# Retention of a two-layer decoder step: last chunk's transposes behind a swish tile, sample state requested earlier, zero-state products left out

## The reference, cut to what matters

```python
def step(s, qkv):
    qc, kc, vc = qkv
    scores = jnp.einsum('bhqd,bhkd->bhqk', qc, kc) * intra
    o = (jnp.einsum('bhqk,bhkv->bhqv', scores, vc)
         + jnp.einsum('bhqd,bhdv->bhqv', qc, s) * q_decay[None, :, :, None])
    s = (s * chunk_decay[None, :, None, None]
         + jnp.einsum('bhkd,bhkv->bhdv', kc * k_decay[None, :, :, None], vc))
    return s, o
...
o = (o - mu) * lax.rsqrt(var + GN_EPS)
o = (o.reshape(B, L, D_RET_V) * jax.nn.silu(g.astype(f32))).astype(h.dtype)
```

## Time and profile before

| | us |
|---|---|
| runs | 2209.39, 2207.01, 2209.02 |
| median | 2209.02 |
| the profiled execution | 2204.35 |
| its span | 2202.5 |
| TensorE busy | 2098.8 (95%) |
| DVE, ACT, POOL busy | 1124.8, 698.2, 338.6 |

### The profile page before, as it was taken

The page is one execution under the profiler, slowest core; times in us unless marked ns, Lnnn a source line. Parts: engine busy times, 40 slices in busy tenths (PEclk is TensorE's granted clock), DMA queues, the critical chain, the costliest instruction groups (busy, mean ns, idle before and its releaser), DMA issues.

```text
span 2202.5 us, 37914 instructions
## 1 busy us (share of the span) xinstructions
PE 2098.8 (95%) x15356; PEld 2007.0 (91%) x15356; DVE 1124.8 (51%) x1706; ACT 698.2 (32%) x896; POOL 338.6 (15%) x314
## 2 busy tenths in 40 slices
PE   5999899989999999999999999989899999999997
PEld 2899889979998999999989998989899989999997
DVE  5534546886345534343456254488743463535343
ACT  2123433455323212121231244325552331212122
POOL 0001102430013101010230010044100310101014
PEclk9999999999999999999999999999999999999998
DMA  8341242222224333333332213422222422222222
GB/s 332 140 176 58 72 161 93 72 71 78 86 82 167 123 117 115 115 115 115 120 139 78 76 53 111 154 72 72 75 79 87 153 68 87 77 87 80 84 87 97
DMA packets 78918, 232.58 MB, mean 106 GB/s; under 512 B 7360, under 2 KB 27840, under 8 KB 78528
## 3 DMA queue, kind: packets, MB, share of 16 engines
q1 hardware_dynamic: 56304, 204.86, 27.2%
q10 hardware_dynamic: 22480, 25.78, 3.5%
HBM read 218.52 MB, written 12.09 MB: 105 GB/s over the span
## 4 chain that ended last, share of the span: by engine, by line
PE 83%; DVE 10%; ACT 3%; issue 2%; DMA 1%; DVEq 1%; ACTq 0%; POOL 0%; POOLq 0%
PE acc L1161 72%; PE misc L1231 2%; PE acc L1212 2%; DVE taps L869 2%; DVE weight_l L691 1%; ACT weight_h L364 1%; PE misc L1241 1%; DVE tmp L921 1%; PE misc L1350 1%; DVE taps L867 1%; PE misc L1324 1%; PE misc L1322 1%; PE misc L1323 1%; PE misc L1388 1%; DVE tmp L886 0%
## 5 line engine op out<-in xcount | busy, mean ns | idle before, releaser
L364 ACT ACTIVATE weight_h<-raw 128x1024 fp32r<-128x1024 f32 x288 | 304.7, 1058 | 1038.8 <-PE acc L1161 997.1
L1161 PE MATMUL acc<-h_hi,weight_h 128*128 128x288 f32 x2688 | 587.7, 300 | 26.0 <-DVE weight_l L691 20.7
L1161 PE MATMUL acc<-h_lo,weight_h 128*128 128x288 f32 x2688 | 578.5, 297 | 0.0
L1161 PE MATMUL acc<-h_hi,weight_l 128*128 128x288 f32 x2688 | 578.2, 297 | 0.0
L691 DVE TENSOR_TENSOR weight_l<-raw,weight_h 128x1024 fp32r<-128x1024 f32 x288 | 400.4, 1390 | 265.2 <-ACT weight_h L364 265.2
L1161 PEld LDWEIGHTS acc<-h_hi,weight_h 128*128 128x128 f32 x2688 | 435.6, 190 | 42.3 <-DVE weight_l L691 27.6
L1161 PEld LDWEIGHTS acc<-h_lo,weight_h 128*128 128x128 f32 x2688 | 436.5, 190 | 0.0
L1161 PEld LDWEIGHTS acc<-h_hi,weight_l 128*128 128x128 f32 x2688 | 436.0, 190 | 0.0
L1161 PE MATMUL acc<-b_hi,weight_h 128*128 128x288 f32 x1792 | 388.8, 299 | 18.5 <-DVE tmp L939 13.7
L1161 PE MATMUL acc<-b_lo,weight_h 128*128 128x288 f32 x1792 | 385.5, 297 | 0.0
L1161 PE MATMUL acc<-b_hi,weight_l 128*128 128x288 f32 x1792 | 385.2, 297 | 0.0
(11 more groups left out here) (207 smaller groups left out, 1759.9 us busy)
## 6 DMA issues: line engine op xcount, KB each, us to landing
raw<-stream SPq DMA_DIRECT2D x290, 512.0 KB, 3.4
ada_raw<-ada_in SPq DMA_DIRECT2D x84, 512.0 KB, 6.0
s_s<-state_in ACTq DMA_DIRECT2D x8, 1024.0 KB, 5.5
ret_s_out<-s_s ACTq DMA_DIRECT2D x8, 1024.0 KB, 4.9
two_raw<-ada_in SPq DMA_DIRECT2D x12, 512.0 KB, 9.3
x<-x_in ACTq DMA_DIRECT2D x1, 2304.0 KB, 12.9
wrg<-wrg_in ACTq DMA_DIRECT2D x18, 128.0 KB, 2.0
const<-const_in SPq DMA_DIRECT2D x1, 1246.0 KB, 8.6
```

The costliest lines, as they stand in the source:

```text
L364: A(weight_h[:, j % 2, :], raw[:, (j + 2) % 4, :], ACT.Copy).then_inc(h_split, 1)
L1161: last = M(acc[j % 2][:, half, 0:HALF], w, r[:, k, half * HALF:(half + 1) * HALF], start=(k == 0 and n == 0), stop=(k == KT - 1 and n == 2))
```

## The change

- `turn_v` of the last V tile moves behind the scores of the first chunk. Tiles 6 and 7 go through `misc` banks 2 and 3 (`v_bank`), so that banks 0 and 1 are free for the scores.
- `turn_o` of the eighth chunk moves behind the first G tile, and ACT's copy of it (`o_evac`) behind the split that follows that tile. `sample_scores` no longer waits for this copy; `sample_updates` does.
- The state `s_p` moves to the bytes of `taps`, `on_p` behind `v_tok`, and the staging tiles into the second half of `s_s`. ACT requests the first sample state at the start of the MA tiles, the second after the second store, and doesn't wait for the stores.
- `kd_s` lies in the bytes of `taps`, so DVE waits for both stores ahead of it. Ahead of that wait, at all even G tiles, stands now `split_l`.
- For the first chunk of each i there is no product with `s_p` (L1323), no zeroing (L792), and the state is a copy in place of two multiply-adds (L806).
- Two loops of DVE and POOL over i are written out.

```diff
@@ -89,6 +89,11 @@
     return buf[:, bass.ds(m, 1), :].rearrange("p o (a b) -> p (o a) b", a=2)
 
 
+def v_bank(j):
+
+    return 2 if j >= 6 else 0
+
+
 def prompt(tile):
     return tile[:, :, 0:HALF_P]
 
@@ -140,17 +145,17 @@
                    enumerate([offs["qk"] + 2 * TOK * 4 + q * 4096 for q in range(3)] + [offs["side"]])]
         two_row = place("two_row", [128, 512], F32, lo + 4 * 4096)
         x_part = place("x_part", [128, 2, NB_S], F32, offs["side"] + 4096)
-        s_p = place("s_p", [128, 2, DV], F32, lo)
-        on_p = place("on_p", [128, 2, DV], F32, lo + 2048)
-        p_m = place("p_m", [128, 2, CHUNK], F32, lo + 4096)
-        kd_p = place("kd_p", [128, 2, DK], F32, lo + 5120)
-        k_st = place("k_st", [128, 2, 2, CHUNK], F32, lo + 6144)
-        q_st = place("q_st", [128, 2, 2, CHUNK], F32, lo + 8192)
+        on_p = place("on_p", [128, 2, DV], F32, offs["tmp"] + 4 * 4096)
+        p_m = place("p_m", [128, 2, CHUNK], F32, lo + 8192)
+        kd_p = place("kd_p", [128, 2, DK], F32, lo + 9216)
+        k_st = place("k_st", [128, 2, 2, CHUNK], F32, lo + 10240)
+        q_st = place("q_st", [128, 2, 2, CHUNK], F32, lo + 12288)
         s_s = place("s_s", [128, 2, DB, DV], F32, lo)
         k_ss = place("k_ss", [128, NB_S], F32, lo + 16640)
         on_s = place("on_s", [128, DV], F32, lo + 16896)
         wrg = place("wrg", [128, 2, 256])
         taps = place("taps", [128, STRIP])
+        s_p = place("s_p", [128, 2, DV], F32, offs["taps"])
         kd_s = place("kd_s", [128, DB // 2, DK], F32, offs["taps"])
         q_sm = place("q_sm", [128, DB * COLS])
         p_ms = place("p_ms", [128, 128])
@@ -452,8 +457,8 @@
                     split_h(lay, AT_V, 0, j)
                     ada_between(AT_V + j)
                     act.wait_ge(v_turned, lay * 8 + j + 1)
-                    A(v_tok[:, :, j * 128:(j + 1) * 128], misc[:, 0, :].rearrange("p (c d) -> p c d", c=4), ACT.Copy)
-                    A(v_s[0:NB_S, j * 128:(j + 1) * 128], misc[0:NB_S, 1, 0:128], ACT.Copy).then_inc(v_ready, 1)
+                    A(v_tok[:, :, j * 128:(j + 1) * 128], misc[:, v_bank(j), :].rearrange("p (c d) -> p c d", c=4), ACT.Copy)
+                    A(v_s[0:NB_S, j * 128:(j + 1) * 128], misc[0:NB_S, v_bank(j) + 1, 0:128], ACT.Copy).then_inc(v_ready, 1)
 
                 def o_evac(i, c, n):
 
@@ -466,6 +471,12 @@
                     act.wait_ge(s_ready, lay * 8 + (i * 4 + 4) + 1)
                     act.dma_start(ret_p_out[bass.ds(lay * 4 + i * 2, 2)].rearrange("h p n -> p h n"), s_p[:]).then_inc(ret_p_stored, 16)
 
+                def load_state(i, e):
+
+                    act.wait_ge(state_stored[e], lay * 32 + i * 16 + 1)
+                    act.dma_start(s_s[:, e], state_in[bass.ds(lay, 1), :, bass.ds(i * 2 + e, 1)].rearrange("l b h p n -> p (l b h) n")).then_inc(state_loaded[e], 16)
+
+                load_state(0, 0)
                 zero = lay * 0
                 for t in range(8):
                     i, c = t // 4, t % 4
@@ -482,23 +493,16 @@
                     A(gstd[:], mv[:, :, 1], ACT.Sqrt, bias=eps_g[:]).then_inc(gstd_ready, 1)
                     if t == 3:
                         store_state(0)
-                o_evac(zero + 1, 3, n)
                 store_state(1)
 
-                act.wait_ge(ret_p_stored, lay * 32 + 32 + 1)
-
-                def load_state(i, e):
-
-                    act.wait_ge(state_stored[e], lay * 32 + i * 16 + 1)
-                    act.dma_start(s_s[:, e], state_in[bass.ds(lay, 1), :, bass.ds(i * 2 + e, 1)].rearrange("l b h p n -> p (l b h) n")).then_inc(state_loaded[e], 16)
-
-                load_state(0, 0)
                 load_state(0, 1)
                 for i in range(2):
                     for j in range(4):
                         e, m = j // 2, i * 4 + j
                         n = lay * 4 + i * 2 + e
                         split_h(lay, AT_G, zero + i, j)
+                        if i == 0 and j == 0:
+                            o_evac(zero + 1, 3, lay * 8 + 7)
                         if i == 0 and j == 3:
                             load_state(1, 0)
                         if i == 1 and j == 1:
@@ -786,10 +790,7 @@
                         V.tensor_copy(dst[:, SEQ:TOK].rearrange("p (a b) -> p a b", a=2), sample(acc[j % 2])).then_inc(acc_free, 1)
                         split_l(lay, AT_V, i, j)
 
-                with dve.Fori(0, 2) as i:
-                    dve.wait_ge(ret_p_stored, lay * 32 + i * 16 + 1)
-
-                    V.memset(s_p[:], 0.0)
+                for i in range(2):
                     for c in range(4):
                         n = lay * 8 + i * 4 + c
                         dve.wait_ge(scores_ready, n + 1)
@@ -802,7 +803,10 @@
                         V.tensor_copy(one(mix, i * 4 + c), acc[c % 2][:, :, 0:HALF]).then_inc(acc_free, 1)
                         split_l(lay, AT_MA, i, c)
                         dve.wait_ge(o_ready, n + 1 + 1)
-                        for e in range(2):
+                        if c == 0:
+                            dve.wait_ge(ret_p_stored, lay * 32 + i * 16 + 1)
+                            last = V.tensor_copy(s_p[:], misc[:, 2, :].rearrange("p (e d) -> p e d", e=2))
+                        for e in range(2 if c else 0):
                             last = V.scalar_tensor_tensor(s_p[:, e, :], s_p[:, e, :], cdec[:, bass.ds(i * 2 + e, 1)], misc[:, 2, e * 256:e * 256 + 256], ALU.mult, ALU.add)
                         last.then_inc(s_ready, 1)
                         ch = Chain(dve, norm_chain, n * 2)
@@ -828,9 +832,12 @@
                             V.tensor_tensor(apart, misc[0:NB_S, 0, 0:NB_S].rearrange("p (s c) -> p s c", c=2 * DS),
                                             mask_s[:, bass.ds(h, 1), :].rearrange("p o (s c) -> p (o s) c", c=2 * DS), ALU.mult)
                             kt = misc[0:NB_S, 0, 128:256].unsqueeze(1).to_broadcast([NB_S, DB // 2, DK])
+                            split_l(lay, AT_G, i, j)
+                            dve.wait_ge(ret_p_stored, lay * 32 + 32 + 1)
                             km = kdm[:, bass.ds(h, 1), :].rearrange("p o b -> p (o b)").unsqueeze(2).to_broadcast([NB_S, DB // 2, DK])
                             V.tensor_tensor(kd_s[0:NB_S], kt, km, ALU.mult).then_inc(s_masked_ready, 1)
-                        split_l(lay, AT_G, i, j)
+                        if j % 2:
+                            split_l(lay, AT_G, i, j)
                         dve.wait_ge(g_sig, lay * 8 + i * 4 + (j + 1))
                         V.tensor_tensor(one(tmp, m), acc[j % 2][:, :, 0:HALF], one(tmp, m), ALU.mult).then_inc(acc_free, 1)
                         ch = Chain(dve, s_chain, n * 2)
@@ -1070,7 +1077,7 @@
                     for n in range(ADA_PROLOGUE, ADA_JOINT):
                         add_bias(n, lay, n * 4, n % 2)
                     pool.wait_ge(tables_loaded, 16)
-                with pool.Fori(0, 2) as i:
+                for i in range(2):
                     for c in range(4):
                         n = lay * 8 + i * 4 + c
                         pool.wait_ge(qk_ready, lay * 8 + 8 + 1)
@@ -1280,9 +1287,10 @@
                     pe.wait_ge(acc_free, n[0] + (j + 3))
                     pe.wait_ge(v_ready, n[1] + j + 1)
                     src = o_t[:, 2 + j % 2, :]
+                    bank = v_bank(j)
                     for c in range(4):
-                        nc.tensor.transpose(misc[:, 0, c * 128:(c + 1) * 128], src[:, c * 128:(c + 1) * 128], ident)
-                    nc.tensor.transpose(misc[0:NB_S, 1, 0:128], src[:, SEQ:TOK], ident).then_inc(v_turned, 1)
+                        nc.tensor.transpose(misc[:, bank, c * 128:(c + 1) * 128], src[:, c * 128:(c + 1) * 128], ident)
+                    nc.tensor.transpose(misc[0:NB_S, bank + 1, 0:128], src[:, SEQ:TOK], ident).then_inc(v_turned, 1)
 
                 n = (lay * LAYER_TILES + AT_V, lay * 8)
                 for j in range(8):
@@ -1290,7 +1298,7 @@
                     if j:
                         turn_v(n, j - 1)
                     ada_between(AT_V + j)
-                turn_v(n, 7)
+                v_base = n
 
                 def turn_o(n):
 
@@ -1301,8 +1309,6 @@
                             last = nc.tensor.transpose(misc[:, 3, (2 * e + half) * 128:(2 * e + half + 1) * 128], on_p[:, e, half * 128:(half + 1) * 128], ident)
                     last.then_inc(on_turned, 1)
 
-                pe.wait_ge(v_ready, lay * 8 + 8 + 1)
-                carry(pe)
                 for i in range(2):
                     for c in range(4):
                         n = lay * 8 + (i * 4 + c)
@@ -1312,22 +1318,26 @@
                             M(misc[:, 0, e * 256:e * 256 + 128], k_st[:, c % 2, e, :], qc, start=True, stop=True)
                             last = nc.tensor.transpose(misc[:, 0, e * 256 + 128:e * 256 + 256], k_st[:, c % 2, e, :], ident)
                         last.then_inc(scores_ready, 1)
+                        if n == lay * 8:
```

(14 more changed lines are left out.)

## The result

The changed kernel takes 2231.47 us (four runs, 2226.68 to 2235.28) against 2208.61 for the kernel before beside it: 1.010 times as long, 95% interval 1.0076 to 1.0124. It is slower by 22.9 us, where 13.4 were forecast. The profiled execution took 2226.68, 22.3 above that of before.

The account below looks back on a forecast made before the run. TensorE was taken to bound the kernel (83% of the chain). Gains -5.4 - 3.5 - 13.7, stalls +24.8 and clock +11.2 give +13.4 on 2204.35: 2217.8, plus 4.67 to the median, forecast 2222, range 2211 to 2234 us.

Parts of the forecast that it names:

- Last V transposes: At the last V tile, scores fill the wait for ACT's `v_s`: gain 1.9 us in layer 0, 3.5 in layer 1.
- Zero state: TensorE's product with the zero state (L1323) goes, 0.43 us eight times: gain 3.5 us.
- Tail: After the eighth chunk, waits and half clock go: 7.35 us left per layer, gain 13.7 us for both.
- The early request at nothing: ACT's first sample state load, requested at the start of the MA tiles, was costed at nothing.
- The stall: At even G tiles `kd_s` comes behind `split_l`, so `sample_o` starts 3.0 us after the tile: eight times, +24.8 us.
- The restart: TensorE's first products after each wait for `kd_s` run slower, making 3.2 us of each 3.0 us gap.
- DVE's later work behind the split: DVE's sigmoid product, statistics and state update come later, but answer to a tile ending 6.4 us after: nothing charged.
- Faster: Rival: the wait for `kd_s` behind `split_l` is only about 2.0 us with no clock fall: 2202 us; chance 0.07.
- The clock: TensorE's clock falls to half behind seven of the eight new waits, at 1.6 us each: +11.2 us.
- the rival of long falls: Every clock fall lasts the longer time, as `sample_o` and updates are small products: 23.2 us, total 2234; chance 0.11.

Follow-up runs that it names:

- the run with the late request: Changed kernel with `kd_s` made ahead of `split_l` again, and the first sample state requested behind the second store: 2191.94 us.
- the run with the wait filled: Changed kernel with three 512-column matmuls, their result overwritten, ahead of each of the eight waits for `kd_s`: 2212.15 us, ratio 1.0019 to the kernel before.
- the version with `kd_s` first: Changed kernel with `kd_s` made ahead of `split_l` at even G tiles again: 2186.47 us, ratio 0.9894 to the kernel before.
- the swap alone: Kernel before with only `split_l` put ahead of `kd_s` at even G tiles: 2257.37 us, ratio 1.0217 to the kernel before.

## Why the prediction was right, and by how much its terms were off

The mechanism and the direction were right; the measured 2231.5 lies within 2211 to 2234, near its upper end. Point by point:

**Last V transposes.** Forecast 1.9 and 3.5 us. The chain of after in layer 0, then in layer 1, against the earlier trace rows:

```profile
180.34 0.12 PE misc L1293
...
182.12 6.38 PE acc L1168 x48
```

```profile
1266.52 0.12 PE misc L1293
...
1268.29 6.38 PE acc L1168 x48
```

From the end of tile 6's transposes to the MA tile 1.66 and 1.65 (forecast 1.58), in place of 3.50 and 4.21, and the MA tile of layer 1 takes 6.38 in place of 7.23. Gain 1.8 and 3.4. Right.

**Zero state.** Eight times 0.43. Right by the rows.

**Tail.** From the eighth chunk's end to the end of `turn_o` 7.31 us in both layers (261.69 to 269.00, 1347.87 to 1355.18), forecast 7.35. Right; taking it back cost 15.8 where 13.7 were put.

**The early request at nothing: wrong.** The step named its cover rightly for the weight tiles, but judged the state's own landing by its 6.7 us being "far earlier than needed" and so priced the move at nothing. The run with the late request shows waits of 2.9 us (5.5 us in all by the medians, not clear of their scatter): the price of a cover that another part of the same change takes away. It didn't alter the sum, as the tail's gain had been booked in full.

**The stall.** Forecast T + 3.0, measured 3.04 six times and 2.61 twice: 23.5 us. The restart was put at 0.2 each; `sample_o`'s first pair takes 0.67 in place of 0.63, so it is 0.04. The term is 23.8 in place of 24.8. DVE's later work behind the split, put at nothing, cost nothing: in the run with the wait filled, the next G tile takes its 6.58.

**A slip without weight.** In the rival *Faster*, eight stalls of 2.0 with `turn_o` in two of them are 15.2, not 15.6.

**The clock: the term that was mis-sized.** Seven falls at 1.6 were put; the profiled execution has six, and their price, as excess over the same rows without a fall (0.67, 1.00, 1.06 and 6.58), is 1.4 at 315, 3.0 at 335, 3.1, 3.1 and 3.1 in layer 1, and 1.6 at 1431: 15.3 in place of 11.2. The step that was mis-sized is "I take the shorter, since TensorE has work at once behind each new stall". The work at once is the small products of `sample_o` and `sample_updates`, and the slow stretch began in or behind them and lasted nearly 7 us in four of six times. That was the rival of long falls, at 0.11; the truth lies between it and the forecast. By medians the term is 19.3 (the filled kernel), which the scatter doesn't tell from 15.3; the changed kernel's profiled execution was the fastest of its four. The Trainium skill's rule on the penalty ("TensorE: Matmul & The Clock Gate", Terms) agrees roughly with these rows: a half of 6.8 is 3.4 where they give 3.0 to 3.1, and a half of 3.4 is 1.7 where they give 1.4 and 1.6.

**What the sum lacked.** -22.6 + 23.8 + 15.3 is 16.5, and the profiled executions differ by 22.3. The stalls and the clock behind them don't lack anything: 23.8 + 15.3 is 39.1, and the changed kernel's profiled execution lies 40.0 above that of the version with `kd_s` first. The missing 5.8 us lie in places that the change doesn't touch. Between two waits of TensorE that both kernels have, one in layer 0 behind the retention and one at the head of layer 1, the kernel before needed 681.7 us (481.94 to 1163.60) and the changed one 684.5 (487.02 to 1171.55). Of these 2.9 us the clock is 0.9: it fell at 1154.6, and the 64 matmuls there take 10.27 in place of 9.33. The other 2.0 go where TensorE multiplies `two_raw`, which took 1.86 before and now 3.9 (1146.0 to 1149.87), with two waits for its DMA in it. From 1171.55 to the first V transposes it is 2.8 more (52.93 in place of 50.17): a fall at 1171.7 costs about 1.7, and for the rest the matmuls, at a granted clock of 1.00, start every 133 ns where they had started every 130. Smaller differences elsewhere, up to 1 us, nearly cancel. Both falls lie behind gaps, 1.77 and 2.58 us, that the kernel before had as well, without a fall. What sets the pace and the landing of the DMA in one execution and not in another stays open. The profiled execution of before was also a fast one, 5.6 us under the median of the later nineteen.

## What to carry to other kernels

Before an instruction is put ahead of another in an in-order queue, ask what that instruction waits for, not what it costs: the split took 1.2 us, but it waited for the end of the very tile under which the small work behind it had been hidden. Price a short wait of TensorE with the clock behind it, by what it does next: behind these waits of 3 us the clock cost from two thirds as much as the waits (15.3 to 23.5, the changed kernel's profile) to as much (24.9 to 24.4, the swap alone). And where two parts of a change remove a wait and a cover at once, cost each with the other in place.

## What the runs showed of the hardware

- Issued matmuls alone didn't hold the clock here. With three matmuls on the whole array in each wait it stayed at 1.00 over both stretches; with three of the same columns and nearly the same duration on a 32 x 32 corner it was granted at 0.92 and 0.84 in the execution that was profiled, with TensorE busy to the same extent.
- The same wait is followed by a fall in one execution and not in another: the 2.40 us wait at 1695 left the clock at 1.00 in one version and was followed by 0.50 in another. The kernel before has some nine waits of 2 to 2.7 us elsewhere, with a fall behind five of them in its profile, and its single runs scatter more than their first sample told (that the one makes the other is likely, not shown): it spanned 2207.0 to 2209.4 in its first three runs and 2196.6 to 2212.4 in nineteen. An edit worth 3 us can't be judged from it without its rows.
